# Rounded head means: each fp32 mean matmul of three projections becomes two rounded matmuls, fed by ScalarE and GpSimd

## What is computed

```python
def l2norm(x):
    return x * lax.rsqrt(jnp.sum(x * x, axis=-1, keepdims=True) + 1e-6)

def rms_norm(x, gain=None):
    xf = x.astype(F32)
    y = xf * lax.rsqrt(jnp.mean(xf * xf, axis=-1, keepdims=True) + EPS)
    if gain is not None:
        y = y * gain.astype(F32)
    return y.astype(x.dtype)

# delta rule: q = l2norm(heads(q)) * GDN_HEAD_DIM ** -0.5; k = l2norm(heads(k))   (heads of 128)
# diff and na: q and k are rms_norm'ed per head of 64; the diff output per head of 128
```

## Time and profile before

| | |
|---|---|
| time, median of 3 runs | 2449.57 us (2448.03 to 2449.85) |
| the profiled execution's span | 2447.7 us |
| TensorE busy | 2394.9 us, 98% of the span |
| VectorE, ScalarE, GpSimd busy | 1495.8, 958.7, 831.6 us |
| chain that ended last, TensorE's share | 84% |
| delta-rule projection, diff projection, na projection | about 133 to 231, 788 to 886 and 970 to 1082 us |

### The profile page before, as it was taken

The page is one execution under the profiler, slowest core; times in us unless marked ns, Lnnn a source line. Parts: engine busy times, 40 slices in busy tenths (PEclk is TensorE's granted clock), DMA queues, the critical chain, the costliest instruction groups (busy, mean ns, idle before and its releaser), DMA issues.

```text
span 2447.7 us, 37094 instructions
## 1 busy us (share of the span) xinstructions
PE 2394.9 (98%) x14385; PEld 1959.5 (80%) x14385; DVE 1495.8 (61%) x2056; ACT 958.7 (39%) x1531; POOL 831.6 (34%) x454
## 2 busy tenths in 40 slices
PE   8999999999999999999999999999999999999999
PEld 6778877888886878866888888888887758788887
DVE  5765755547666976585466766644778586524242
ACT  4566644232224645356342222122266332423232
POOL 2533033544442222233223323223234313354443
PEclk9999999999999999999999999999999999999999
DMA  7212023445441110120224434323311111232322
GB/s 251 87 63 84 3 69 119 138 147 180 138 142 39 61 35 20 52 76 2 69 95 137 147 120 138 113 94 95 129 65 47 61 60 61 86 112 95 101 97 86
DMA packets 64662, 227.41 MB, mean 93 GB/s; under 512 B 7040, under 2 KB 9088, under 8 KB 63882
## 3 DMA queue, kind: packets, MB, share of 16 engines
q1 hardware_dynamic: 51160, 176.05, 21.5%
q10 hardware_dynamic: 13362, 49.40, 6.1%
HBM read 223.30 MB, written 2.12 MB: 92 GB/s over the span
## 4 chain that ended last, share of the span: by engine, by line
PE 84%; DVE 7%; issue 4%; ACT 3%; POOL 2%; DMA 0%; SPq 0%; DVEq 0%; POOLq 0%; ACTq 0%
PE ps L277 23%; PE ps L278 23%; PE ps L279 23%; PE ps L1064 2%; PE ps L1324 2%; POOL w_lo L3401 1%; PE ps L1286 1%; DVE rstd L963 1%; PE ps L1081 1%; PE ps L1094 1%; PE ps L1304 1%; PE ps L362 1%; PE ps L361 1%; PE ps L360 1%; PE ps L3173 1%
## 5 line engine op out<-in xcount | busy, mean ns | idle before, releaser
L3401 POOL TENSOR_TENSOR w_lo<-ring,w_hi 128x1024 fp32r<-128x1024 f32 x288 | 703.9, 2444 | 1167.2 <-ACT w_hi L270 664.6
L277 PE MATMUL ps<-act_hi,w_hi 128*128 128x512 f32 (+1 forms) x2280 | 844.0, 370 | 8.5 <-DVE act_lo_mixer L605 2.9
L279 PE MATMUL ps<-act_hi,w_lo 128*128 128x512 f32 (+1 forms) x2280 | 829.7, 364 | 0.0
L278 PE MATMUL ps<-act_lo_ffn,w_hi 128*128 128x512 f32 (+1 forms) x1408 | 513.6, 365 | 0.0
L277 PEld LDWEIGHTS ps<-act_hi,w_hi 128*128 128x128 f32 x2280 | 430.0, 189 | 95.3 <-issue 13.8
L279 PEld LDWEIGHTS ps<-act_hi,w_lo 128*128 128x128 f32 x2280 | 429.3, 188 | 72.0
L270 ACT CAST w_hi<-ring 128x1024 fp32r<-128x1024 f32 (+1 forms) x167 | 172.7, 1034 | 627.1 <-PE ps L279 569.3
L1715 ACT CAST w_hi<-ring 128x1024 fp32r<-128x1024 f32 (+1 forms) x132 | 137.5, 1044 | 456.9 <-PE ps L279 456.9
L278 PEld LDWEIGHTS ps<-act_lo_ffn,w_hi 128*128 128x128 f32 x1408 | 265.6, 189 | 41.0
L1604 DVE SCALAR_TENSOR_TENSOR ada_place<-ada_place 128x1024 f32<-128x1024 f32 x180 | 279.8, 1554 | 24.5 <-DMA ada_place<-in_w_ada 10.1
L277 PE MATMUL ps<-hidden_hi,w_hi 128*128 128x512 f32 (+1 forms) x704 | 256.5, 364 | 1.8 <-DVE hidden_lo L1801 1.5
(11 more groups left out here) (465 smaller groups left out, 3224.7 us busy)
## 6 DMA issues: line engine op xcount, KB each, us to landing
ring<-in_w_ffn SPq DMA_DIRECT2D x204, 512.0 KB, 3.3
ada_place<-in_w_ada ACTq DMA_DIRECT2D x90, 512.0 KB, 4.2
ring<-in_w_gdn SPq DMA_DIRECT2D x16, 512.0 KB, 3.3
ring<-in_w_hy SPq DMA_DIRECT2D x12, 512.0 KB, 3.3
ring<-in_w_dil_qk SPq DMA_DIRECT2D x8, 512.0 KB, 8.7
ring<-in_w_out SPq DMA_DIRECT2D x8, 512.0 KB, 3.2
ring<-in_w_diff_qk SPq DMA_DIRECT2D x8, 512.0 KB, 3.3
ring<-in_w_na_qk SPq DMA_DIRECT2D x8, 512.0 KB, 3.3
```

Source lines behind the costliest of these rows:

```text
L277: pe.matmul(out, w[0], x[0], start=start, stop=False)
L278: pe.matmul(out, w[0], x[1], start=False, stop=False)
L279: return pe.matmul(out, w[1], x[0], start=False, stop=stop)
L3401: pool.tensor_tensor(k.w_lo[:, a % SPLITS, :], k.ring[:, a % SLOTS, :], k.w_hi[:, a % SPLITS, :].bitcast(F32), ALU.subtract).then_inc(k.lo ...
```

## The change

The mean matmuls are rounded ones too. ScalarE squares as before, waits for its own result, and copies it rounded to `squares_hi` (one more ScalarE instruction per tile, which raises a new semaphore, `head_squares_hi`). GpSimd subtracts it from the square into `squares_lo` (in the place of `sq`) and now raises `head_squares`, on which TensorE waits. TensorE multiplies both parts with a rounded mean matrix from `means`, which ScalarE fills once with three copies ahead of the delta-rule projection: two fp32r matmuls in place of one fp32 matmul. GpSimd's list of weight rests is written out for these stages, with the rests of squares in it: behind the unit's weight rest in the ordinary slots, in front of it in the values units.

```diff
--- before.py
+++ after.py
@@ -175,10 +175,13 @@
         self.pair_probs = [self.probs.rearrange("p s n -> p (s n)"), self.over(ada_at, "pair_probs", 2 * T)]
         self.hy_odd = self.over(ada_at + 4 * 4 * T, "hy_odd", 4 * S)
         self.pair_turned = self.over(ada_at + 4 * 2 * T, "pair_turned", 4 * T)
+        self.squares_hi = self.over(ada_at + 4 * 4 * T, "squares_hi", 2 * T, R32).rearrange("p (s n) -> p s n", s=2)
+        self.squares_lo = self.over(ada_at, "squares_lo", 2 * T, R32).rearrange("p (s n) -> p s n", s=2)
         self.consts = self.place("consts", NCONST)
         self.mod_flat = self.place("mod", 2 * 96)
         self.mod = self.mod_flat.rearrange("p (l n s) -> p l n s", l=2, s=2)
         self.small = self.place("small", 128)
+        self.means = self.place("means", 3 * P, R32).rearrange("p (s n) -> p s n", s=3)
         self.ps = ctx.enter_context(nc.psum_tensor("ps", [P, 8 * 512], F32))
         self.sems = {}
         self.slot_landed = [self.sem(f"slot_landed_{i}") for i in range(SLOTS)]
@@ -893,9 +896,9 @@
                 pe.wait_ge(self.squares, self.b + j + 1)
                 if j >= 1:
                     pe.wait_ge(self.rooted, self.b + j)
-                last = pe.matmul(k.bank(6), mean, k.sq[:, j % 2, 0:S], start=True, stop=True)
-                if size > S:
-                    last = pe.matmul(k.bank(7, size - S), mean, k.sq[:, j % 2, S:size], start=True, stop=True)
+                for out, a, b in ((k.bank(6), 0, S), (k.bank(7, size - S), S, size)):
+                    pe.matmul(out, mean, k.squares_hi[:, j % 2, a:b], start=True, stop=False)
+                    last = pe.matmul(out, mean, k.squares_lo[:, j % 2, a:b], start=False, stop=True)
                 last.then_inc(self.summed, 1)
 
     def scalar(self, s):
@@ -910,7 +913,8 @@
             src = k.ps[:, 1024 * (i % 3):1024 * (i % 3) + size] if i < n else x
             if i >= 2:
                 s.eng.wait_ge(self.summed, self.b + i - 1)
-            s.eng.activation(k.sq[:, i % 2, 0:size], src, ACT.Square).then_inc(self.squares, 1)
+            link(s, s.eng.activation(k.sq[:, i % 2, 0:size], src, ACT.Square))
+            s.eng.copy(k.squares_hi[:, i % 2, 0:size], k.sq[:, i % 2, 0:size]).then_inc(k.sem("head_squares_hi"), 1)
 
         def keep(i):
 
@@ -947,6 +951,29 @@
         s.eng.activation(k.small[:, 118:119], k.par("one"), ACT.Exp)
         values_out(k, s, self.values, self.dst, s.eng.copy, 0 if self.alone else 1, 1 if self.alone else 2, "values_kept_act")
         split_ahead(k, s, FIRST[self.values] + self.units + SPLITS)
+
+    def gpsimd(self, pool, lower_unit):
+        k, n, u0 = self.k, self.tiles, FIRST[self.name]
+
+        def lower_square(i):
+            if i >= len(self.jobs):
+                return
+            size = self.jobs[i][0].shape[-1]
+            pool.wait_ge(k.sem("head_squares_hi"), self.b + i + 1)
+            pool.tensor_tensor(k.squares_lo[:, i % 2, 0:size], k.sq[:, i % 2, 0:size], k.squares_hi[:, i % 2, 0:size].bitcast(F32),
+                               ALU.subtract).then_inc(self.squares, 1)
+
+        for i, events in enumerate(self.slots):
+            if i < n:
+                lower_unit(u0 + i + SPLITS)
+            if i <= n:
+                lower_square(i)
+            for j in events:
+                if j >= n - 1:
+                    lower_square(j + 2)
+            if n <= i < n + self.units - 1:
+                lower_unit(u0 + i + SPLITS)
+        lower_unit(u0 + n + self.units - 1 + SPLITS)
 
     def vector(self, v):
         k, n = self.k, self.tiles
@@ -2042,17 +2069,17 @@
 
     q, key, val = attn_views(k)
     return Projection(k, "w_na_qk", 8, "w_na_v", 4, HALF, val, 16, 8, 8, jobs=
-                      [(q[:, t, :], k.const("heads64"), k.par("na_q_down"), "eps_query", float(HD), None) for t in range(4)]
-                      + [(key[:, t, :], k.const("heads64"), k.par("na_k"), "eps", 1.0, None) for t in range(4)]
-                      + [(k.mix[:, t, :], k.const("heads128"), k.par("subln"), "eps_subln", SUBLN, None)
+                      [(q[:, t, :], k.means[:, 0, :], k.par("na_q_down"), "eps_query", float(HD), None) for t in range(4)]
+                      + [(key[:, t, :], k.means[:, 0, :], k.par("na_k"), "eps", 1.0, None) for t in range(4)]
+                      + [(k.mix[:, t, :], k.means[:, 1, :], k.par("subln"), "eps_subln", SUBLN, None)
                          for t in range(4)])
 
 
 def diff_project(k):
     q, key, val = attn_views(k)
     return Projection(k, "w_diff_qk", 8, "w_diff_v", 4, HALF, val, 8, 0, 0, jobs=
-                      [(q[:, t, :], k.const("heads64"), k.par("da_q"), "eps_query", float(HD), k.par("da_q_swap")) for t in range(4)]
-                      + [(key[:, t, :], k.const("heads64"), k.par("da_k"), "eps", 1.0, k.par("da_k_swap")) for t in range(4)])
+                      [(q[:, t, :], k.means[:, 0, :], k.par("da_q"), "eps_query", float(HD), k.par("da_q_swap")) for t in range(4)]
+                      + [(key[:, t, :], k.means[:, 0, :], k.par("da_k"), "eps", 1.0, k.par("da_k_swap")) for t in range(4)])
 
 
 GQA = 28
@@ -2493,8 +2520,9 @@
             pe.wait_ge(k.sem("head_squares"), j - 1)
             if j >= 4:
                 pe.wait_ge(k.sem("head_rooted"), j - 3)
-            pe.matmul(k.bank(5 + 2 * (j % 2)), k.const("ones"), k.sq[:, j % 2, 0:S], start=True, stop=True)\
-                .then_inc(k.sem("head_summed"), 1)
+            out = k.bank(5 + 2 * (j % 2))
+            pe.matmul(out, k.means[:, 2, :], k.squares_hi[:, j % 2, 0:S], start=True, stop=False)
+            pe.matmul(out, k.means[:, 2, :], k.squares_lo[:, j % 2, 0:S], start=False, stop=True).then_inc(k.sem("head_summed"), 1)
 
     dense_tensor(k, pe, "w_gdn", 16, k.h_hi, k.lo1, (S,), k.sem("gdn_taps"), behind=behind, stored=k.pairs["dil"].all_stored())
 
@@ -2510,7 +2538,8 @@
         if j < 8:
             if j >= 2:
                 s.eng.wait_ge(k.sem("head_summed"), j - 1)
-            s.eng.activation(k.sq[:, j % 2, 0:S], x[:, j, :], ACT.Square).then_inc(k.sem("head_squares"), 1)
+            link(s, s.eng.activation(k.sq[:, j % 2, 0:S], x[:, j, :], ACT.Square))
+            s.eng.copy(k.squares_hi[:, j % 2, 0:S], k.sq[:, j % 2, 0:S]).then_inc(k.sem("head_squares_hi"), 1)
 
     def root(j):
 
@@ -3432,12 +3461,23 @@
     for stage, values, units in (("dil", "w_dil_v", 4), ("diff", "w_diff_v", 4), ("na", "w_na_v", 4),
                                  ("gqa", "w_gqa", 6)):
         if stage == "diff":
-            lower_units(done, FIRST["w_ffn1"] + SPLITS)
+            lower_units(done, FIRST["w_gdn"] + SPLITS)
+            for j in range(16):
+                lower(FIRST["w_gdn"] + j + SPLITS)
+                if 1 <= j <= 8:
+                    pool.wait_ge(k.sem("head_squares_hi"), j)
+                    pool.tensor_tensor(k.squares_lo[:, (j - 1) % 2, 0:S], k.sq[:, (j - 1) % 2, 0:S],
+                                       k.squares_hi[:, (j - 1) % 2, 0:S].bitcast(F32), ALU.subtract).then_inc(k.sem("head_squares"), 1)
+            lower_units(FIRST["w_gdn"] + 16 + SPLITS, FIRST["w_ffn1"] + SPLITS)
             added_beside(k, pool, k.view(k.big, 0, DT, S), 0)
             lower_units(FIRST["w_ffn1"] + SPLITS, FIRST["w_diff_qk"] + SPLITS)
             added_beside(k, pool, ffn1(k).total, DT // 2)
             done = FIRST["w_diff_qk"] + SPLITS
-        lower_units(done, FIRST[values] + units + SPLITS)
+        if stage in ("diff", "na"):
+            project = (diff_project if stage == "diff" else na_project)(k)
+            project.gpsimd(pool, lambda u: lower_units(u, u + 1))
+        else:
+            lower_units(done, FIRST[values] + units + SPLITS)
         done = FIRST[values] + units + SPLITS
         k.pairs[stage].gpsimd(pool)
     lower_units(done, UNITS)
@@ -3534,6 +3574,8 @@
     k.pairs["dil"].scalar(s, lambda p: dil_between_scalar(k, s, p))
     mark("dil_attend")
     act.wait_ge(k.loaded_late, 48)
+    for i, name in enumerate(("heads64", "heads128", "ones")):
+        act.copy(k.means[:, i, :], k.const(name))
     gdn_project_scalar(k, s)
     gdn_masks_scalar(k, s)
     gdn_products_scalar(k, s)
```

## The result

| | before | after |
|---|---|---|
| time, median of 21 runs each | 2449.57 us (2448.03 to 2450.99) | 2452.38 us (2451.61 to 2456.41) |
| ratio, 95% interval | | 1.0016, 1.0010 to 1.0022 |
| profiled execution, span | 2447.7 us | 2450.1 us |
| mean granted clock | 0.997 | 0.995 |

The account below looks back on a forecast made before the run. TensorE, 98% busy, was taken as the bound, tied with ScalarE in the delta rule and VectorE at na's end. Delta rule 4.4, clock 1.7, diff -2.0 and na -2.7 sum to +1.4 us: 2451.0 us, range 2446 to 2457.

Parts of the forecast that it names:

- TensorE's saving: Across the 28 means: each saves 0.40 us at 512 columns, 0.59 at 768; 15.0 us if all on the path.
- What is added: Per mean: ScalarE's copy about 0.65 us (512 columns) or 0.9 (768), GpSimd's rest 1.27 or 1.8, each handover 0.1.
- Delta rule: Delta-rule projection: late mean 0 and ScalarE slots of 6.8 us cost +4.4 us, plus 1.7 for a clock fall.
- Two signs that I had named: Delta-rule projection: each mean from 2 to 7 waits for GpSimd, and unit 10 begins about 4 to 6 us later.
- Diff: Diff projection: mean 0 costs +2.2 us, means 1 to 7 give -4.1, no VectorE loss, no clock fall counted: -2.0 us.
- na: na projection: VectorE's end -3.3 us, TensorE's -4.4; a clock fall behind mean 8's pause makes TensorE's the later, -2.7.
- (1): Whole kernel: nearly all of TensorE's 15.0 us arrives, 2434.5 us; chance 0.10 together with a halfway case at 2442.
- (2): Diff and na's tail: VectorE stands still more while GpSimd works, +7.6 us, 2457 us; chance 0.22.
- The dearest case of rival 2: na's tail: VectorE's scaling meets a square's rest and the weight rest right behind it, losing up to 4.2 us twice.
- (3): All means: a rounded matmul is as slow as the fp32 one, so nothing is gained, 2461 us; chance under 0.02.
- The sum: Whole kernel: 4.4 + 1.7 - 2.0 - 2.7 = +1.4 us, giving 2451.0 us.

Follow-up runs that it names:

- e4: Changed kernel without ScalarE's copies and GpSimd's rests of squares, the rounded square multiplied twice (rests missing from the means): 2435.30 us, ratio 0.9948 to before.
- e3: Changed kernel with fp32 matmuls on constants filling three of TensorE's four pauses: 2448.92 us, ratio 1.0000 to before.
- e6: Changed kernel with ScalarE's copies but without GpSimd's rests of squares, rounded squares used twice: 2444.93 us, ratio 0.9979 to before.
- e7: Changed kernel with delta rule as before, late means of diff and na inside TensorE's units, ScalarE's and GpSimd's na orders changed: 2437.44 us, ratio 0.9952 to before.
- e10: Changed kernel with delta rule as before, late means inside TensorE's units, ScalarE's and GpSimd's na orders as in the change: 2440.56 us, ratio 0.9966 to before.
- e1: Changed kernel with the delta-rule projection as before, diff and na rounded: 2446.03 us, ratio 0.9989 to before.
- e5: Changed kernel with the delta-rule means, roots and scalings one unit later: 2449.56 us, ratio 1.0001 to before.
- e9: Changed kernel with the delta-rule means and the transposes of the gates each one unit later: 2447.55 us, ratio 0.9995 to before.
- e8: Changed kernel with delta-rule means one unit later and late means of diff and na inside TensorE's own work: 2440.24 us, ratio 0.9964 to before.

## Why the prediction was right, point by point

**TensorE's saving: right.** 0.23 us a matmul (202.52 to 202.75), steps in diff 9.09 us where 9.1 was put. e4 shows that 12.0 us of the 15.0 can arrive in the three stages.

**What is added: right.** The copy of 768 columns takes 0.84 us (I took 0.80 and 0.9 in all), that of 512 0.62. The rest of 512 columns takes 1.27 us and that of 768, which no row of before had, 1.85 where 1.8 was put. Row of after, one line's instructions, duration in ns min/median/max:

```profile
L963 POOL TENSOR_TENSOR squares_lo<-sq,squares_hi x20: 1802/1846/2707, 797.2 to 1067.4; 128x768 fp32r<-128x768 f32 x20
```

**Delta rule: right in its mechanism, +6.1 put, +6.9 found.** Without falls of the clock +4.4 was put and e3 shows +4.6. Slots are 6.8 us and slot 7 8.63, the pause for mean 0 is 3.79 us where 3.8 was put. Missed was a second long pause, 2.41 us in front of mean 6: it lies in slot 7, where the exponentials of the gates make the square 1.9 us later still; I had these 1.9 us in ScalarE's sum, but had not asked what TensorE does meanwhile. A fall of the clock is behind it too. The two falls cost 2.3 us where 1.7 was put: 1.6 the first, 0.7 the second, which ScalarE's slots partly hide. Two signs that I had named came out otherwise: means 3 to 6 wait for GpSimd (0.23, 0.58, 0.57 and 2.41 us), not 2 to 7 (e3, without the falls, has the wait at mean 7 too, 0.60 us), and unit 10 begins 6.9 us later in its stage, where I had put 4 to 6. That only the last link, the rest, is named in the waits must not be read as its being the cause: by e4, e6 and after, the copies are 6.3 us of the 8.9 between e4 and after, the rests 2.6.

**Diff: the term that failed, -2.0 put, +0.4 found.** The pause, 3.23 us, was right (3.3). But the sum counted a fall of the clock only at the longest two pauses and put the third at nothing, for no better reason than its length; it had one, and e3 shows that it cost 1.6 us. A second thing was left out of the sum: ScalarE's copy of square 7 makes the evacuation of tile 7 later, and the values wait 0.61 us for its bank (e7, where `keep` goes ahead, has no such wait, and e10, where it does not, is 0.8 us longer). Some 0.2 us stay unexplained; mean 0 came 2.75 us later in its stage, as put (2.8). VectorE was not the bound, as forecast: it ends 3.78 us ahead of the values' copies, where it was 5.07.

**na: right, -2.7 put, -2.6 found.** The pause of 3.98 us (4.1 put) has its fall. VectorE's row, for which I had put -3.3, ends with TensorE: it waits 1.70 us at 1065.81 for a root whose mean comes late behind that fall. e1, e5 and e9 bear it out: with the same instructions the clock stays low for 6.8 us there and not 3.4, and the same wait is 2.96, 3.04 and 2.75 us. The stage is then at -1.4, -1.3 and -1.6 us, so that agreement to 0.1 us is in part luck: it is that of an execution with the short stretch.

**The rivals.** (1) The whole of TensorE's saving did not arrive, and e4 with e6 shows why: in the three stages 9.7 us go to the copies and 7.0 to the rests. (2) VectorE's standing still did not become worse in na. Its scalings lose 0.6 and 1.0 us in the row, 1.6 in all against 2.1 before. That depends on how the two engines happen to meet: in e3, with the same code in na, the row's first scaling takes 2.43 us as well, 3.0 lost in all, and the wait for the root shrinks to 0.38 us. The rule that I cited from the Trainium skill ("SBUF — State Buffer", section "Who interferes with whom": the one that issues second waits for the whole instruction) agrees with what the traces show, in both directions. In e10 VectorE's scaling at 1053.26 begins inside GpSimd's rest and ends at 1054.84, 0.81 us after it, and the weight rest that GpSimd has ready at 1053.98 then takes 3.11 us and not 2.4. That is also the answer to what I had left open there: the waiting VectorE got its turn between two GpSimd instructions that stood back to back. The dearest case of rival 2, 4.2 us twice, needed it to be passed over. In diff it is larger than in na, but falls on one tile: L967 of before lost some 0.6 us at each of eight tiles (1.27 us in the median, 0.69 when alone); at tile 0 of after VectorE's L847, L848, L994 and L995 take 3.18, 2.23, 2.19 and 2.06 us where they take 1.16, 0.69, 0.69 and 0.48 at later tiles, 6.6 us lost in all, but VectorE is ahead there and the stage does not pay. There too it got its turn between a weight rest (from 801.37) and a rest of a square (from 803.84). (3) A rounded matmul takes 0.23 us. The price that I gave this rival was wrong: with a rounded matmul as slow as the fp32 one the means would cost twice as much, 8 x 0.86 + 20 x 1.29 = 32.7 us more and not 11.

**The sum** came within 1.4 us of the time, better than its terms, and that is luck. The stages gave 4.7 us (6.9 + 0.4 - 2.6) where 1.4 was put; the profiled span hides 1.8 of it in the first stage and 0.7 in the last. By the ratio the change costs 3.9 us, 2.4 to 5.4 by its interval, so the forecast of +1.4 was too good by 1 to 4 us, which is the fall in diff and the stages' small terms. That the kernel did not become faster came from the tie of ScalarE with TensorE in the delta rule, as put: e1, without the change in that stage, is 2.7 us below before by the ratio.

## What to carry to other kernels

A cheaper instruction on the busiest engine is worth what the chain in front of it lets through: add up the new links (here copy 0.65 and rest 1.37 us) against how long the input has been ready, mean by mean, and also in the one unit where another engine has extra work. If the input is late, move the consumer into the middle of the engine's own work before making it cheaper, and then look for the next thing that the old pause covered (here the transposes of the gates). Order the feeding engine by who waits: a root or an evacuation that frees a bank goes ahead of a square that nobody needs yet.

## What the runs showed of the hardware that I had not expected

Behind pauses of 3.79, 3.98, 3.23 and 2.41 us between dense matmuls TensorE was granted 0.50, the 1.2 GHz level, for 3.4 us. Shorter ones differ: behind 2.70 us the clock fell in e5 and stayed in e8, which has the same instructions there, and behind 1.69 and 1.91 us (e7) and 2.11 us (e4) it stayed. At 2.12 us for a weight rest it is the other way round: e8 has a fall behind it (at 197.6 us), e5 none behind its 2.13. And it fell behind less: behind 1.54 us in e9, and behind 1.38 and 1.10 us close together in e10 (at 1053.0). So the length of a pause does not alone decide it, and a forecast should carry a fall behind a pause over 2 us as likely, not only behind the longest. What a fall costs depends on who paces: 1.6 us in diff and behind mean 0 of the delta rule, 0.7 behind mean 6, nothing where ScalarE's slots cover it (e8, e9). In na the stretch at half clock is 3.4 us long in after and 6.8 in e1, e5 and e9 with the same instructions, and the stage is 1.0 to 1.4 us longer there.

Also unexpected was that GpSimd pays as well as VectorE: rests of 1.8 us took up to 2.71 us (at 803.84 in after, while VectorE's L847 ran to 804.83), and a weight rest of 2.4 us took 3.11 us, as above, where VectorE's scaling had its turn first.
